# Narrow products woven between wide ones, and attention scores handled in the order fourth, third, first, second query block

## The reference

```python
s = ql @ c.T + qr @ kr.T          # latent part, 128 deep, and rotary part, 64 deep
s = s * ks[:, h] * scale          # one scale per key and head
s = where(k_pos <= q_pos, s, -1e30)
p = softmax(s)
o = (p @ c) @ w_uv[h]             # then one shared output projection w_o
```

## Time and profile before

| | us |
|---|---|
| median of 3 runs | 2068.43 (2066.1 to 2071.49) |
| the profiled execution, its time | 2071.82 |
| the profiled execution, its span | 2070.0 |
| TensorE busy | 2046.9 |
| VectorE busy | 1606.2 |
| ScalarE busy | 1127.8 |
| GpSimd busy | 366.0 |

### The profile page before, as it was taken

One profiled execution on the slowest core, in us unless ns is written; L12 is line 12 of the kernel. 1 busy time (PEld: TensorE's weight loads), 2 busy tenths in 40 slices (PEclk: granted clock), 3 DMA queues, 4 the chain that ended last, 5 costly groups with the idle time before them and its releaser, 6 DMA issues.

```text
span 2070.0 us, 44517 instructions
## 1 busy us (share of the span) xinstructions
PE 2046.9 (99%) x16756; PEld 1997.7 (97%) x16756; DVE 1606.2 (78%) x2687; ACT 1127.8 (54%) x1955; POOL 366.0 (18%) x437
## 2 busy tenths in 40 slices
PE   9999999999999999999999999999999999999998
PEld 8999999999999999999999999998789899999998
DVE  6779985427366998988899898769675578989997
ACT  5446554433224665655665565556585556656555
POOL 0011111122011111111111111113242221111111
PEclk9999999999999999999999999999999999999999
DMA  5467783232325777776677777443322126777775
GB/s 161 119 161 179 190 200 108 84 100 65 100 65 128 176 179 178 183 179 157 161 187 182 177 180 184 122 136 99 94 78 80 59 69 157 181 189 179 186 174 130
DMA packets 362556, 295.71 MB, mean 143 GB/s; under 512 B 22103, under 2 KB 327556, under 8 KB 362148
## 3 DMA queue, kind: packets, MB, share of 16 engines
q1 hardware_dynamic: 325498, 227.26, 37.0%
q0 software_dynamic: 36592, 66.07, 19.1%
q10 hardware_dynamic: 314, 0.37, 0.1%
HBM read 224.57 MB, written 2.66 MB: 110 GB/s over the span
## 4 chain that ended last, share of the span: by engine, by line
PE 81%; DMA 7%; DVE 7%; issue 3%; ACT 2%; SPq 1%; DVEq 0%; ACTq 0%
PE main L810 25%; PE side L859 25%; PE main L859 18%; DMA raw<-raw 3%; DMA sums_w<-raw 2%; DVE w_lo L2184 2%; PE side L1418 2%; PE main L1321 1%; DMA raw<-in_ffn_w_up 1%; PE main L1162 1%; DMA raw<-in_ffn_w_down 1%; PE main L1331 1%; PE side L1377 1%; PE side L1250 1%; PE side L1078 1%
## 5 line engine op out<-in xcount | busy, mean ns | idle before, releaser
L859 PE MATMUL side<-xw_hi,w_hi 128*128 128x260 f32 x1344 | 381.1, 284 | 4.9 <-DVE tmp_in L2333 2.2
L859 PE MATMUL side<-xw_hi,w_lo 128*128 128x260 f32 x1344 | 381.0, 283 | 0.0
L859 PE MATMUL side<-xw_lo,w_hi 128*128 128x260 f32 x1344 | 380.1, 283 | 0.0
L2184 DVE TENSOR_TENSOR w_lo<-raw,w_hi 128x512 fp32r<-128x512 f32 (+2 forms) x472 | 323.4, 685 | 41.7 <-ACT w_hi L1548 22.4
L859 PE MATMUL main<-xw_hi,w_hi 128*128 128x260 f32 x1008 | 286.1, 284 | 0.0
L859 PE MATMUL main<-xw_lo,w_hi 128*128 128x260 f32 x1008 | 284.7, 282 | 0.0
L859 PE MATMUL main<-xw_hi,w_lo 128*128 128x260 f32 x1008 | 284.5, 282 | 0.0
L859 PEld LDWEIGHTS side<-xw_hi,w_hi 128*128 128x128 f32 x1344 | 253.2, 188 | 8.2 <-DVE tmp_in L2333 4.2
L859 PEld LDWEIGHTS side<-xw_hi,w_lo 128*128 128x128 f32 x1344 | 253.1, 188 | 0.0
L859 PEld LDWEIGHTS side<-xw_lo,w_hi 128*128 128x128 f32 x1344 | 252.8, 188 | 0.0
L3122 POOL DMA_DIRECT2D sums_w<-raw x116 | 101.0, 871 | 696.8 <-DMA raw<-in_ffn_w_gate 318.0
(11 more groups left out here) (470 smaller groups left out, 5439.7 us busy)
## 6 DMA issues: line engine op xcount, KB each, us to landing
sums_w<-raw POOLq DMA_DIRECT2D x112, 256.0 KB, 3.3
raw<-raw POOLq DMA_DIRECT2D x112, 256.0 KB, 5.2
raw<-in_ffn_w_gate SPq DMA_DIRECT2D x86, 256.0 KB, 4.4
raw<-in_ffn_w_gate SPq DMA_DIRECT2D x43, 512.0 KB, 6.1
raw<-in_ffn_w_up SPq DMA_DIRECT2D x84, 256.0 KB, 4.3
raw<-in_ffn_w_up SPq DMA_DIRECT2D x42, 512.0 KB, 6.3
raw<-in_gmlp_w_in SPq DMA_DIRECT2D x16, 1024.0 KB, 5.4
raw<-in_ffn_w_down SPq DMA_DIRECT2D x56, 256.0 KB, 3.9
```

Of the source, the lines that this page charges most:

```text
L859: mm = nc.tensor.matmul(into[j], w_tiles(w, weights_at(s, j))[:, k, :], moving[:, k, order[j], :], start=(j in (0, 1) and k == 0 and i == ...
L2184: a = nc.vector.tensor_tensor(dst, src, hi.bitcast(F32), ALU.subtract)
```

## The change

There are three edits to the order of work, and no product, scaling or copy is added or left out.

- `SCALED = (3, 2, 0, 1)` is the order of the query blocks in the rotary products, in VectorE's scaling and in the masks. VectorE waits for two scored blocks ahead of blocks 3 and 2, and for all four ahead of blocks 0 and 1. A mask product waits for its own block's place in that order.
- `mask_scores` with `free` waits for the evacuation ahead of every block, not of blocks 0 and 2 alone.
- `weigh` makes key block 0 first, and when a head follows, weaves the three latent products of that head's query block 0 (128 columns) between its three products (512 columns). They stood in `latent_scores(h + 1, (0, 1))` ahead of it. Then the products of key blocks 1 (384 columns) and 3 (128 columns) alternate, and key block 2 (256 columns) comes last.

```diff
--- before.py
+++ after.py
@@ -495,6 +495,7 @@
 
             return 2 * (u // 3) + min(u % 3, 1) + 1
 
+        SCALED = (3, 2, 0, 1)
         P_AT = [0, 1, 3, 6]
         PROB_PARTS = ((1, 8 * P, 2 * P), (2, 0, 4 * P), (3, 4 * P, 4 * P))
         PT_AT = [0, 4, 8, 7]
@@ -1302,12 +1303,18 @@
                 for q in blocks:
                     if h == 0 and q == 0:
                         pe.wait_ge(sd_set, 3)
-                    if free is not None and q % 2 == 0:
+                    if free is not None:
                         pe.wait_ge(evac_done, free - 1 + q // 2)
                     if h >= 1:
-                        pe.wait_ge(score_scaled, QB * (h - 1) + q + 1)
+                        pe.wait_ge(score_scaled, QB * (h - 1) + SCALED.index(q) + 1)
                     nc.tensor.matmul(main[:, q // 2, q % 2, q * P:(q + 1) * P], mask_ops[:, 0, :], mask_ops[:, 1, :],
                                      start=True, stop=False, skip_group_check=True)
+
+            def latent_product(h, q, i):
+
+                queries, keys = ((q_hi[:, h % 2], c_hi), (q_hi[:, h % 2], c_lo), (q_lo[:, h], c_hi))[i]
+                nc.tensor.matmul(main[:, q // 2, q % 2, 0:(q + 1) * P], queries[:, q * P:(q + 1) * P], keys[:, 0:(q + 1) * P],
+                                 start=False, stop=False, skip_group_check=True)
 
             def latent_scores(h, blocks):
                 if h == 0:
@@ -1315,14 +1322,12 @@
                     pe.wait_ge(key_parts_set, 2)
                 pe.wait_ge(q_lo_set, h + 1)
                 for q in blocks:
-                    bank = main[:, q // 2, q % 2, :]
-                    nk, cols = (q + 1) * P, slice(q * P, (q + 1) * P)
-                    for a, b in ((q_hi[:, h % 2, cols], c_hi), (q_hi[:, h % 2, cols], c_lo), (q_lo[:, h, cols], c_hi)):
-                        nc.tensor.matmul(bank[:, 0:nk], a, b[:, 0:nk], start=False, stop=False, skip_group_check=True)
+                    for i in range(3):
+                        latent_product(h, q, i)
 
             def rope_scores(h):
                 pe.wait_ge(qr_moved_set, h + 1)
-                for q in (0, 1, 3, 2):
+                for q in SCALED:
                     nk = (q + 1) * P
                     if q in (0, 3):
                         lo, q_rope = ROPE * (h % 2), qr[:, h // 2, q * P:(q + 1) * P]
@@ -1357,7 +1362,7 @@
                                           ks_all[:, blk, 32 * g:32 * g + 32], pieces[2 * i + blk // 4][:, blk % 4, 0:KL],
                                           start=False, stop=(blk == NP - 1 and odd == 1), skip_group_check=True)
             mm.then_inc(os_done, 1)
-            mask_scores(1, range(QB))
+            mask_scores(1, SCALED)
             latent_scores(1, range(QB))
             rope_scores(1)
             pe.wait_ge(o_rows_set, 1)
@@ -1407,16 +1412,27 @@
                 turn(g, (0,), 2)
                 turn(g, (1, 3), 3)
 
-            def weigh(g):
+            def weigh_product(g, k, i):
+
+                c, p = ((rows_hi, prob_hi), (rows_hi, prob_lo), (rows_lo, prob_hi))[i]
+                return nc.tensor.matmul(side[:, 2, k * P:SEQ], c[:, k, :], p[:, PT_AT[k] * P:(PT_AT[k] + QB - k) * P],
+                                        start=(k == 0 and i == 0), stop=(k == 2 and i == 2), skip_group_check=True)
+
+            def weigh(g, following=None):
 
                 if g == 0:
                     pe.wait_ge(c_lo_set, 2)
-                for k, part in ((0, 2), (1, 3), (3, 3), (2, 3)):
-                    pe.wait_ge(head_lo_set, 4 * g + part)
-                    cols = slice(PT_AT[k] * P, (PT_AT[k] + QB - k) * P)
-                    for i, (c, p) in enumerate(((rows_hi, prob_hi), (rows_hi, prob_lo), (rows_lo, prob_hi))):
-                        mm = nc.tensor.matmul(side[:, 2, k * P:SEQ], c[:, k, :], p[:, cols], start=(k == 0 and i == 0),
-                                              stop=(k == 2 and i == 2))
+                pe.wait_ge(head_lo_set, 4 * g + 2)
+                for i in range(3):
+                    weigh_product(g, 0, i)
+                    if following is not None:
+                        latent_product(following, 0, i)
+                pe.wait_ge(head_lo_set, 4 * g + 3)
+                for i in range(3):
+                    weigh_product(g, 1, i)
+                    weigh_product(g, 3, i)
+                for i in range(3):
+                    mm = weigh_product(g, 2, i)
                 mm.then_inc(pv_done, 1)
 
             def out_step(m, k):
@@ -1434,7 +1450,7 @@
             for h in range(1, H):
                 g = h - 1
                 if g == KC + 1:
-                    mask_scores(h, range(QB), free=e)
+                    mask_scores(h, SCALED, free=e)
                     latent_scores(h, range(QB))
                 elif h > 1:
                     latent_scores(h, (2, 3))
@@ -1442,12 +1458,14 @@
                     rope_scores(h)
                 turns(g)
                 if g != KC and h + 1 < H:
-                    mask_scores(h + 1, range(QB))
+                    mask_scores(h + 1, SCALED)
                 if g >= 1:
                     values(g - 1, turned=True)
                 if g != KC and h + 1 < H:
-                    latent_scores(h + 1, (0, 1))
-                weigh(g)
+                    latent_scores(h + 1, (1,))
+                    weigh(g, h + 1)
+                else:
+                    weigh(g)
                 if g == KC:
                     pe.wait_ge(score_scaled, QB * (h + 1))
                     for i in range(4):
@@ -3040,8 +3058,8 @@
                     dve.wait_ge(key_scale_in[h % 2], 16 * (h // 2 + 1))
                     if h >= 2:
                         dve.wait_ge(prob_turned, 3 * (h - 1))
-                    for q in range(QB):
-                        dve.wait_ge(scored, QB * h + (2 if q < 2 else QB))
+                    for q in SCALED:
+                        dve.wait_ge(scored, QB * h + (2 if q >= 2 else QB))
                         nk = (q + 1) * P
                         nc.vector.tensor_tensor_reduce(prob[:, h % 2, P_AT[q] * P:P_AT[q] * P + nk], main[:, q // 2, q % 2, 0:nk],
                                                        key_scale[:, h % 2, 0:nk], 1.0, -3.0e38, ALU.mult, ALU.max,
```

## The result

| | before | changed |
|---|---|---|
| median of 6 runs, us | 2068.3 (2066.1 to 2071.49) | 2076.94 (2074.32 to 2083.97) |
| profiled execution, time | 2071.82 | 2083.97 |
| its span | 2070.0 | 2082.4 |
| from the stage's first mask load to its last output load | 190.3 | 197.4 |

The ratio is 1.0041 with a 95% interval from 1.0029 to 1.0052, 8.6 us between the medians. The changed kernel is slower. A second set of runs, on the same chip as some of the experiments, gave 1.0033 (1.0021 to 1.0045).

The account below looks back on a forecast made before the run. TensorE was taken as the bound, its last mask product waiting for VectorE's last scaled piece. 6.0 + 0.34 + 0.3 + 0.1 = +6.8 us gave 2075.2 us for the median (2078.6 for the profiled execution); range 2070.2 to 2078.3.

Parts of the forecast that it names:

- Weaving, taken at 0: Probability products: a narrow product still costs its 0.11 us beside wide ones, so weaving gains 0.
- rival A: Weaving pays: wide neighbours hide the narrow products' weight loads, 4.5 us back, total +2.3 us; chance 0.10.
- Scaling starts 0.43 later: Rotary products: long blocks go first, so VectorE's scaling starts at 1.30 in place of 0.87 us.
- Rival B: Not slower: rotary passes run at 0.46 ns a column, scaling starts at 0.91, total +1.3 us; chance 0.10.
- C: Rotary passes queue, so scaling starts after 1.4 us; 2.9 us more, total time 2078 us; chance 0.10.
- Same scaling, same tail: Four scaled pieces still take 1.74 us; last mask loads 0.05 after them, value products 0.19 after that.
- 14 heads at 0.43, 6.0 us: Heads 2 to 15: each period grows 0.43 us because TensorE waits for VectorE's later scaling; 6.0 us.
- step 7: Head 10's masks: two more stand behind the evacuation wait, at most 0.10 us each; +0.1 us.
- Head 1, +0.34: Head 1: block 0's three latent products, moved behind the probability products' wait, are not hidden; +0.34 us once.
- Head 0, +0.3: Head 0: VectorE's small copy behind the scaling, and TensorE's products with it, come later; +0.3 us once.

Follow-up runs that it names:

- weave_only: Changed kernel's weaving alone, with the block orders and evacuation waits of the kernel before; ratio to the kernel before 0.9997.
- short_then_long: Changed kernel without weaving, block order 0, 2, 3, 1, block 0 scaled after one scored block, block 2 after two; ratio to the kernel before 0.9986.
- short_long_short: Same as short_then_long, but head 10's evacuation waits only ahead of blocks 0 and 2, as in the kernel before; ratio to that kernel 0.9993.
- late_scaling: Kernel before, with VectorE waiting for all four scored blocks before it scales the first; ratio 1.0055.
- early_scaling: Kernel before, with VectorE scaling block 0 once one block is scored, in place of two; ratio 1.0003.

## Why the prediction was right

The forecast was +6.8 us and slower; the medians are 8.6 apart, 6.9 in the second set of runs, and the stage 7.1. By its steps:

1. *Weaving, taken at 0.* Shown by weave_only and by the loads in the trace after. The rival A at 4.5 us less is out.
2. *Scaling starts 0.43 later.* It was 0.46 (0.88 to 1.34). The end of block 3's second pass was right to 0.01, and what was short is the step from there to VectorE: 0.22 where the old order had 0.16. Rival B (a start at 0.91) and C (passes that queue, a start beyond 1.4) are both out. The rotary products ended at 1.35, so nothing waited for block 0 to start first, or it cost nothing: block 1's first pass started at 1569.15, before block 0's at 1569.36. C was priced too low by its own working: half of its 0.66 is 0.33, and 14 x 0.33 makes 4.6 us more, 2079.8, above the range, where 2.9 and 2078 were put down. As C did not occur, the forecast's middle doesn't hang on it. The rule of the Trainium skill ("TensorE: Matmul & The Clock Gate", section "The mechanism") that products start in program order does not hold here across row groups.
3. *Same scaling, same tail.* Right: 1.73 us of scaling, 0.05 to the mask, 0.19 to the values.
4. *14 heads at 0.43, 6.0 us.* The 12 periods with a mask grew by 0.44 on average, 5.3 in all. Head 9's grew by 0.77 and the part from head 15 on by 0.42. Together 6.4, of which 0.3 belong to step 7. That leaves 6.1, a little under 14 x 0.46, most of all because head 3's period grew by 0.29 alone.
5. *Head 1, +0.34.* Measured +0.32 in the changed kernel, +0.34 in weave_only. In steady heads the wait of the probability products was met in time, as worked out: their period with and without weaving is the same.
6. *Head 0, +0.3.* Measured +0.34: the copy is at 1504.64 and the loads with it at 1504.99, both behind the scaling.
7. *Head 10's masks, +0.1.* This term was mis-sized. It is about 0.3. In the kernel before, two of the masks were loaded 1.1 us ahead of the other two; now all four stand behind the later evacuation. Each has a wait of its own, and the four loads come 0.07 to 0.13 apart (merged below, 0.42 for the four) where two waits let them follow 0.02 apart. The waits alone are priced by short_then_long and short_long_short, whose three last masks load 0.07 and 0.13 apart with a wait of their own each and 0.02 and 0.06 apart without: 0.05 to 0.07 more between the loads for a wait that is already met, and 0.08 for the whole period (55.10 and 55.02).

```profile
1629.81 0.42 PEld L1310 LDWEIGHTS main<-mask_ops 128*128 128x128 bf16 x4 [1.12 <-DVE x L2199]
```

The sum is 7.1 against 6.8. What the prediction did not see is that the old order was balanced. It named VectorE's start as what binds; the end of the rotary products bound just as much, and that is why only a later start showed. It said that TensorE's wait at the last mask has no slack, and did not say that the next wait on the same chain lies 0.2 us behind it.

One thing stays open: why the step from the last rotary record to VectorE is 0.16 in one order and 0.22 in others. In late_scaling it was 0.22 too, in early_scaling 0.08 (1.35 to 1.43) for the very same condition, all four blocks scored by the same program of TensorE, and in short_then_long 0.04 for block 2. VectorE had stood for 1.07 and 1.32 us where the step was 0.22, for 0.55 where it was 0.16, and for about 0.1 where it was 0.08 and 0.04. So it goes with how long VectorE had stood, but nothing here shows why. The records' ends are modelled, and no run here parts the signal from the model.

## What to carry to other kernels

A narrow product costs as much as a weight load wherever it stands, if only one load is ahead; look at the distances between weight loads behind wide products before weaving. Where one engine feeds another piece by piece, order the pieces so that the consumer starts early and then never stands: here a short one first, then the long ones. (Whether the last should be short was not tested by itself.) Long first makes it start late, and every later step of the chain inherits that. And after removing a wait, look for the next wait on the same chain before pricing the gain.

## What was not expected of the hardware

In these traces weight loads are not pulled further ahead than one, even where the product in flight takes 0.24 us and a load needs 0.11. Two row groups of the array run apart from each other's order: block 1's pass, last in the program, started, by the records, 0.21 us before block 0's. A semaphore wait ahead of a small product, already met, put its load 0.05 to 0.07 us further from the one before (the masks of head 10 in short_then_long against short_long_short). A VectorE instruction started 0.22 us after the record of the product that it waited for when VectorE had stood for over 1 us, and 0.08 after it when it had stood for 0.12.
